# Encoder and decoder blocks in one kernel: conversions of the dilated stage in another order, cross attention without a row of token scales, its output in three split passes, squares taken earlier

## The reference, cut to what matters

```python
def first_block(x, mem, ...):                      # one layer
    q, k, v, u, y = split(rmsnorm(h, norm_mix_g) @ w_in)
    attn = dilated_mixture_attention(rope(q), rope(k), v)         # 8 heads of 64
    rec = bidirectional_rglru(conv(u), ...) * gelu(y)
    h = h + concat([attn, rec]) @ w_out
    h = h + memory_cross_attention(rmsnorm(h, norm_cross_g), rmsnorm(mem, norm_mem_g),
                                   w_cq, w_ck, w_cv, w_co)        # 4 heads of 128
    h = h + square(relu(rmsnorm(h, norm_mlp_g) @ w_mlp_in)) @ w_mlp_out
    return rmsnorm(h, norm_final_g)

def second_block(x, ...):                          # two layers
    o_mla, o_fnet, o_diff, o_hgrn = four mixers of rmsnorm(x, ln_mix) @ w_in
    x = x + (sum over n of sigmoid(gate_n) * (o_n @ w_branch[n])) @ w_out
    x = x + (silu(g) * u) @ w_down                 # g, u of rmsnorm(x, ln_ffn) @ w_gate_up
```

## Time and profile before

| | |
|---|---|
| median of three runs | 1317.44 us (1315.93 to 1322.8) |
| the profiled execution, its own time | 1320.47 us |
| its span in the profile | 1318.7 us |
| mean granted TensorE clock | 0.992 |
| TensorE busy | 1276.7 us, 97% of the span |
| VectorE busy | 863.5 us, 65% |
| ScalarE busy | 641.5 us, 49% |
| GpSimd busy | 116.6 us, 9% |
| DMA | 211.77 MB, mean 161 GB/s |

### The profile page before, as it was taken

How to read it: one execution, slowest core, us unless ns; L and a number is a source line. 1 busy time by engine, 2 the same in 40 slices (tenths; PEclk the granted TensorE clock), 3 DMA queues, 4 the chain that set the end, 5 groups by cost and what they waited for, 6 DMA issues and landing times.

```text
span 1318.7 us, 22038 instructions
## 1 busy us (share of the span) xinstructions
PE 1276.7 (97%) x9196; PEld 1179.6 (89%) x9196; DVE 863.5 (65%) x1206; ACT 641.5 (49%) x1027; POOL 116.6 (9%) x152
## 2 busy tenths in 40 slices
PE   8988989999999999999999999999999999999998
PEld 8986959998888889998999998898899988999986
DVE  6878547664466756799655554557576996655543
ACT  5865436553366655252364443548553433644432
POOL 2100100000000000481200000000002820000000
PEclk9998999999999999999999999999999999999999
DMA  9532515555543333342545555444334325455552
GB/s 374 212 105 97 192 36 208 202 181 187 184 170 144 140 117 131 130 157 79 209 160 183 179 185 189 166 154 150 106 130 155 133 96 185 143 186 190 192 192 96
DMA packets 30324, 211.77 MB, mean 161 GB/s; under 512 B 3344, under 2 KB 3728, under 8 KB 5264
## 3 DMA queue, kind: packets, MB, share of 16 engines
q1 hardware_dynamic: 29936, 210.22, 44.6%
...
q10 hardware_dynamic: 288, 0.14, 0.0%
...
## 4 chain that ended last, share of the span: by engine, by line
PE 70%; DVE 15%; ACT 8%; issue 6%; DMA 1%; DVEq 0%; ACTq 0%
PE bank L477 68%; DVE w_lo L1545 3%; ACT w_hi L1066 2%; DVE W L1519 2%; ACT W L1066 1%; DVE xs L2035 1%; PE bank L577 1%; ACT x_hi L1066 1%; DVE W L1505 1%; DMA ring<-weight_pieces 1%; DVE W L2015 1%; DVE junk L2033 1%; DVE W L1506 1%; PE bank L783 1%; DVE W L1537 0%
## 5 line engine op out<-in xcount | busy, mean ns | idle before, releaser
L1545 DVE TENSOR_TENSOR w_lo<-ring,w_hi 128x2048 fp32r<-128x2048 f32 (+1 forms) x181 | 418.1, 2310 | 294.8 <-ACT w_hi L1066 294.6
L1066 ACT ACTIVATE w_hi<-ring 128x1024 fp32r<-128x1024 f32 (+1 forms) x364 | 362.1, 1045 | 239.8 <-PE bank L477 224.0
L477 PE MATMUL bank<-x_hi,w_hi 128*128 128x256 f32 x1840 | 266.2, 283 | 2.7 <-ACT w_hi L1066 2.6
L477 PE MATMUL bank<-x_hi,w_lo 128*128 128x256 f32 x1840 | 261.1, 280 | 1.5 <-DVE w_lo L1545 0.9
L477 PE MATMUL bank<-x_lo,w_hi 128*128 128x256 f32 x1840 | 254.2, 280 | 0.0
L477 PEld LDWEIGHTS bank<-x_hi,w_hi 128*128 128x128 f32 x1840 | 236.2, 188 | 5.8 <-issue 2.9
L477 PEld LDWEIGHTS bank<-x_hi,w_lo 128*128 128x128 f32 x1840 | 235.9, 188 | 2.8 <-DVE w_lo L1545 1.7
L477 PEld LDWEIGHTS bank<-x_lo,w_hi 128*128 128x128 f32 x1840 | 233.1, 188 | 0.0
L477 PE MATMUL bank<-W 128*128 128x128 f32 (+4 forms) x716 | 113.4, 327 | 13.3 <-ACT W L1066 8.9
L477 PEld LDWEIGHTS bank<-W 128*128 128x128 f32 (+3 forms) x716 | 88.5, 187 | 28.2 <-issue 13.8
L477 PE MATMUL bank<-w_hi,hid_hi 128*128 128x512 f32 x304 | 78.5, 394 | 0.0
...
## 6 DMA issues: line engine op xcount, KB each, us to landing
...
```

Source lines behind the costliest of these rows:

```text
L477: return nc.tensor.matmul(out, lhsT, rhs, start=first, stop=last)
L1066: return nc.scalar.activation(out, in_, ACT.Copy, scale=scale)
L1545: v.tensor_tensor(w_lo[:, q % SPLITS, 0:n], raw(pp)[:, 0:n], w_hi[:, q % SPLITS, 0:n].bitcast(F32), ALU.subtract).then_inc(s_weight_low, 1)
```

## The change

1. Dilated stage. The low part of `v0`, and both parts of `mem_hi`, move ahead of `rgA 0`; the high part of `v1` stands behind `rgA 0`. `mem_lo` is made in two halves (`memlow`), one before the low part of `v1`, one before that of `ck0`. `memrs` moves behind head 0's mask and maximum. The conversions of `ck1`, `cv0`, `cv1` and `wout0` are each placed in the filler ahead of the projection in front of them, and `rgS`, `rgC 1` and `rgC 3` move to the end of their turn, behind these conversions. The multiplications of the probabilities move from VectorE to ScalarE (two copies with a scale).
2. Cross attention. No row of scales, no multiplication of `cq` by it: the scale of a token, with the constant, is the scale of the exponential and of the maximum. The two `cq` tiles are copied out of PSUM by ScalarE. The scores of heads 0 and 1 are made between the halves of `cq1`, and the four heads follow in an order written out by hand.
3. `co`. Both pieces are split like the others, the values are split into `x_hi` (ScalarE) and `x_lo` (VectorE), and each product is made in three passes of fp32r instead of one in float32: 48 multiplications of 128x512 for 16.
4. Squares. For the norms after `wout` and `co`, the squares of a column block of `h` are taken during the next projection; only the last block's stay behind the norm.
5. In the second block, the row of scales of `ln_ffn` is made behind `gu1` and not between its halves.

```diff
+                late = []
                 if filler and i >= first:
-                    steps.extend(filler.pop(0))
+                    now = filler.pop(0)
+                    if None in now:
+                        now, late = now[:now.index(None)], now[now.index(None) + 1:]
+                    steps.extend(now)
                 if not long:
                     steps.extend(turn)
                 if 3 <= i:
                     steps.append(("value", *heads[i - 3]))
+                steps.extend(late)
...
-        steps += [("low", k[1][-1]), ("rgI",), k[0], ("high", v[0][-1]), ("rgA", 0), k[1], ("high", v[1][-1]), ("rgA", 1), v[0], ("low", v[1][-1])]
         (ck0, ck1), (cv0, cv1) = proj("ck"), proj("cv")
-        steps += [("norm", "norm_mem_g"), ("high", ck0[-1]), ("low", ck0[-1]), v[1], ("memrs",)]
+        wouts = proj("wout", js=range(4))
+        steps += [("low", k[1][-1]), ("rgI",), k[0], ("high", v[0][-1]), ("low", v[0][-1]), ("norm", "norm_mem_g"), ("rgA", 0), k[1], ("memlow", 0)]
+        steps += [("high", v[1][-1]), ("low", v[1][-1]), v[0], ("high", ck0[-1]), ("memlow", 1), ("low", ck0[-1]), ("rgA", 1), v[1]]
         attend([("dil", n) for n in range(8)],
-               [[("rgB", 0), ck0], [("rgB", 1), ("rgS",)], [ck1], [("rgC", 0)], [("rgC", 1), cv0], [("rgC", 2)], [("rgC", 3), cv1], [("mix",)]], 1)
+               [[("memrs",)], [("high", ck1[-1]), ("rgB", 0), ("low", ck1[-1]), ck0], [("rgB", 1), None, ("rgS",)],
+                [("high", cv0[-1]), ("low", cv0[-1]), ck1], [("rgC", 0)], [("high", cv1[-1]), ("low", cv1[-1]), cv0, None, ("rgC", 1)],
+                [("rgC", 2)], [("high", wouts[0][-1]), ("low", wouts[0][-1]), cv1, None, ("rgC", 3)], [("mix",)]])
         mixes = (0, 1, "rec", 2, 3)
-        steps += proj("wout", js=range(4))
+        steps += wouts
         steps.append(("norm", "norm_cross_g"))
         steps += proj("cq")
-        attend([("cross", n) for n in range(4)])
-        steps += proj("co", n=0)
+        cross = lambda kind, n: (kind, "cross", n)
+        steps += [cross("score", 0), cross("score", 1), cross("prob", 0), ("cqcopy",), cross("turn", 0), cross("prob", 1), cross("score", 2),
+                  cross("turn", 1), cross("value", 0), cross("score", 3), cross("prob", 2), cross("value", 1), cross("turn", 2),
+                  cross("prob", 3), cross("value", 2), cross("turn", 3), cross("value", 3)]
+        steps += proj("co")
         steps.append(("norm", "norm_mlp_g"))
         ups = proj("up", js=range(16))
         steps += [*ups[:4], ("params",), *ups[4:]]
...
-                    middle = {"y0": "norm_mix_g", "cq1": "norm_cross_g", "gu1": f"ln_ffn_{l}"}.get(f"{name}{j}")
-                    if middle:
+                    if (name, j) == ("y", 0):
                         def between():
-                            rstd_row(middle)
+                            rstd_row("norm_mix_g")
+                    elif (name, j) == ("cq", 1):
+                        def between():
+                            for n in ("cq.0", "ck.0", "ck.1"):
+                                wait_drained(pe, n)
+                            scores([(ATT["cross", n][1], "cross", n, 0) for n in range(2)])
...
                     elif name == "co":
...
-                        plain(job, "g", at(A_CO, 4, S), loaded(p).rearrange("p (k c) -> p k c", k=4), range(4), 512, p)
+                        q = split_of[p]
+                        hi, lo = (w[:, q % SPLITS, :].rearrange("p (k c) -> p k c", k=4) for w in (w_hi, w_lo))
+                        pe.wait_ge(s_weight_high, 2 * (q + 1))
+                        for tt in range(TT):
+                            bank = fill(f"{job}.{tt}", "g")
+                            for i in range(2):
+                                for kk in range(4):
+                                    if j == tt == i == 0:
+                                        pe.wait_ge(s_co_high, kk + 1)
+                                    elif j == tt == 0:
+                                        wait_drained(pe, f"value.cross{kk}")
+                                    for w, x in ((hi, x_hi), (lo, x_hi)) if i == 0 else ((hi, x_lo),):
+                                        if w is lo and tt == kk == 0:
+                                            wait_low(pe, q)
+                                        ins = mm(bank[:, :], x[:, kk, tt * P:(tt + 1) * P], w[:, kk, :], i == kk == 0 and w is hi, i == 1 and kk == 3)
+                            full(ins, f"{job}.{tt}")
+                        last_job[p] = f"{job}.{TT - 1}"
...
+                    elif name == "gu" and j == 1:
+                        rstd_row(f"ln_ffn_{l}")
...
+                    if phase == "cross" and hd == 2:
+                        wait_drained(pe, "cq.1")
...
+                        if hd % 2 == 0:
+                            scores([(a0, phase, hd, 0), (a0 + 1, phase, hd + 1, 0)])
+                    elif phase != "cross" or hd >= 2:
+                        scores([(a0 + j, phase, hd, j) for j in range(count)])
...
                 elif p in split_of:
-                    split_ahead(p)
+                    split_ahead(p, step[1] not in ("ck", "cv"))
...
+                        squares(stat_name, {"norm_cross_g": (3,), "norm_mlp_g": (1,), "ln_ffn_0": (3,), "ln_ffn_1": (3,)}.get(stat_name, range(4)))
...
+                elif kind == "cqcopy":
+                    drains(copy(at(A_CQ, 4, S)[:, 2:4, :], bank2(wait_filled(act, "cq.1"))), "cq.1")
+                elif kind == "prob" and step[1] == "dil":
+                    a = ATT["dil", step[2]][1]
+                    p0, rs = at(A_SC1 + 512 * (a % 4), TT, S), col(f"rsum{a % 16}", TT)
+                    act.wait_ge(s_dil_recip, a + 1)
+                    copy(p0[:, 0, :], p0[:, 0, :], rs[:, 0:1])
+                    copy(p0[:, 1, :], p0[:, 1, :], rs[:, 1:2]).then_inc(s_prob, 1)
                 elif kind == "proj":
                     _, name, l, j, _ = step
                     job = job_of(name, l, j)
+                    if name == "wout" and j:
+                        squares("norm_cross_g" if l is None else f"ln_ffn_{l}", (j - 1,))
+                    elif name == "co" and j:
+                        squares("norm_mlp_g", (0,))
+                    elif name == "cq" and j == 0:
+                        drains(copy(at(A_CQ, 4, S)[:, 0:2, :], bank2(wait_filled(act, job))), job)
...
+                            token = col("rs.cross.scaled", TT)[:, qt:qt + 1] if phase == "cross" else scale
+                            ins = nc.scalar.activation(sc[:, qt, :], src[:, qt, :], ACT.Exp, bias=nm[:, qt:qt + 1], scale=token, accum_out=sm[:, qt:qt + 1])
...
-                        drains(copy(at(A_CO, 4, S)[:, hd, :], wait_filled(act, name)[:, 0:S]), name)
+                        copy(x_hi[:, hd, :], wait_filled(act, name)[:, 0:S]).then_inc(s_co_high, 1)
...
+                elif kind == "memlow":
+                    gain = vec[:, V_GAIN + GAINS.index("norm_mem_g") * KT:][:, 0:KT]
+                    for j in (2 * step[1], 2 * step[1] + 1):
+                        dve.wait_ge((s_norm_high, s_norm_high_dve)[j % 2], 2 + j // 2 + 1)
+                        for k in (2 * j, 2 * j + 1):
+                            ins = v.scalar_tensor_tensor(mem_lo[:, k, :], mem_t[:, k, :], gain[:, k:k + 1], mem_hi[:, k, :].bitcast(F32), ALU.mult, ALU.subtract)
+                        ins.then_inc(s_norm_low, 1)
...
+                        if name == "norm_cross_g":
+                            dve.wait_ge(s_rs, rs_of[name])
+                            link(v.tensor_scalar(col("rs.cross.scaled", TT), rs, 128.0 ** -0.5, None, ALU.mult))
...
+                    before = {"ck": "norm_mem_g", "f": f"ln_mix_{l}", "gu": f"ln_ffn_{l}"}.get(name)
+                    if before and j == (name == "gu"):
...
-                    elif name == "cq" and j == 1:
-                        for job in ("cq.0", "cq.1"):
-                            scale(at(A_CQ, 4, S)[:, 2 * int(job[-1]):2 * int(job[-1]) + 2, :])
...
+                elif kind == "value" and step[1] == "cross":
+                    hd = step[2]
+                    dve.wait_ge(s_co_high, hd + 1)
+                    bank = wait_filled(dve, f"value.cross{hd}")
+                    drains(v.tensor_tensor(x_lo[:, hd, :], bank[:, 0:S], x_hi[:, hd, :].bitcast(F32), ALU.subtract), f"value.cross{hd}")
...
+                            if phase == "cross":
+                                v.tensor_tensor(nm, mx, col("rs.cross.scaled", TT), ALU.mult).then_inc(s_max, 1)
...
+                    if phase == "dil":
+                        ins.then_inc(s_dil_recip, 1)
+                        continue
```

84 lines of the change are left out of this document (30 added, 54 removed).

## The result

The changed kernel takes 1327.15 us in the median of six runs (1325.71 to 1328.91), the kernel before 1317.28 beside it: ratio 1.0067, 95% interval 1.0046 to 1.0088, 9.9 us slower. Measured a second time, beside experiments and on another chip, it is 1.0056 (1.0034 to 1.0078), 7.4 us. The forecast was 1322.7 us, +5.3, with the range 1310 to 1329. The range holds and the sign is right. The size is too small, and the result lies beyond the half per cent, for which I had the chance 0.36 and not the largest one.

A forecast was written before the change was run, and what follows sets the result against it. TensorE, busy 97% of the span, bounds the kernel, with a ScalarE-VectorE ring pacing the dilated stage. Terms 9.9 - 5.2 - 3.0 + 3.6 = +5.3 us on the median 1317.4 gave 1322.7 us, range 1310 to 1329.

The forecast's parts named there:

- v1 and ck0: Start of the dilated stage: new wait of 0.9 us at v1, then ck0 without its 2.43 wait, ending 3.4 earlier.
- The gain is given back by 102: Dilated stage: TensorE, ahead by 3 us, waits for head 2's probabilities and starts head 1's values at 101.9 instead of 101.42.
- The ring: ScalarE and VectorE releasing each other in the dilated stage: head 6's mask 3.5 us late, last reciprocal 6.3, wout0 7.4.
- The sum of the stage: Whole dilated stage, late start of wout0 plus half clock: +9.9 us, between +7.4 and +11.5.
- Cross attention: Cross attention and co together: co starts 2.6 us earlier and itself takes 2.6 less, -5.2 us, between -7 and -3.5.
- one wait of 1.5 at head 2: Cross attention: the four heads run as before, with a single TensorE wait of 1.5 us, at head 2.
- Rows of `ln_ffn`: Row of scales in two layers: ready once made behind gu1, so the 1.5 us waits go, -3.0 us.
- Banks: Shifted bank rotation: new waits at the start of down (1.6 us) and each wd (1.0, twice), +3.6 us.
- Squares at nothing: Squares during wout and co: two more per projection on ScalarE cost nothing; without that cover about 1 us per block.
- break even: Rival: the dilated stage costs nothing because the ring has unseen slack; 1312.8 us, chance 0.20.
- nor gain: Rival: half-clock stretches and the wait at ck0 go from the dilated stage with nothing replacing them; 1308.9 us, chance 0.14.
- the clock case: Rival: dilated-stage waits leave TensorE at 1.2 GHz into wout0 and delay cv0; 1326.2 us, up to 1329, chance 0.20.

The follow-up runs named there:

- e5: Changed kernel with scans ahead of the conversions, probability scalings on VectorE and the old bank rotation, all put back: 1313.70 us, ratio 0.9952 to the kernel before.
- e7: e5 with the conversions of cv0, cv1 and wout0 one place further back: 1309.70 us, ratio 0.9917 to the kernel before.
- e1: Changed kernel with the dilated stage of the kernel before, the rest as changed: 1317.82 us, ratio 0.9986 to the kernel before.
- e2: Changed kernel with the third and last groups' scans ahead of the conversions of cv1 and wout0 again: 1320.88 us, ratio 1.0012 to the kernel before.
- e3: Changed kernel with the scalings of the dilated stage's probabilities on VectorE again: 1323.20 us, ratio 1.0026 to the kernel before.
- e8: Changed kernel with all squares behind their norms again: 1331.15 us, ratio 1.0090 to the kernel before.
- e4: Changed kernel with the rotation of the shared banks put back by one step ahead of up: 1322.64 us, ratio 1.0019 to the kernel before.

## Why the prediction was right, and where it was short

Times from the mark; first traces, where nothing else is said.

**v1 and ck0: right.** A new wait at `v1` of 0.68 us (0.9 forecast), first scores 1.1 us later (0.9), `ck0` without a wait. **The gain is given back by 102: right**, with the wait of 3.32 for about 3. I named the cause (`memrs` and the scalings) only in part: e5 shows that it is lost even with the scalings away, and e7 that it is kept once the conversions of `cv0`, `cv1` and `wout0` stand further back. At the low one of `cv0` VectorE stands for 8.17 us in the changed kernel (5.26 before).

**The ring: right.** Less the 1.8 of the start, head 6's mask is 3.9 us late (3.5 forecast), the last reciprocal 6.8 (6.3). `wout0` starts 8.7 late; the forecast is the ring's 7.4 and 1.9 for the last value products at half clock, 9.3. Those products cost 0.8 (2.65 us from start to start for 1.82), and the half clock in `wout0` 1.2 (0.6). So the ring was put too short and its clock too dear, by about half a us each, and the two cancel. The sum of the stage, forecast 9.9: 9.9 to `wout0`'s third pass (126.29 for 116.39), 9.5 by e1, and 8.7 in the second pair of traces (126.30 for 117.56). That one of them is 9.9 to the tenth is luck. e2 and e3 measure its two causes at 6.9 and 5.4 alone. They are not independent (12.3 in all), at least since each takes the half clock in `wout0`, 1.2, with it.

**Cross attention, forecast -5.2: -4.2.** `co` itself took 11.39 us (11.2). The step that was short is "one wait of 1.5 at head 2": there are five, 0.48, 0.54, 1.12, 0.75 and 0.75, so `co` starts 1.8 us earlier against `wout0`'s third pass and not 2.6 (47.43 us for 49.19, second traces; the first have 47.41 for 49.95, of which 0.8 is a slower `wout`, see the last section). That the scales come earlier and are needed is right: e8 takes it away and loses 3.0.

**Rows of `ln_ffn`, forecast -3.0: right**; the waits of 1.52 are gone in both layers. **Banks, forecast +3.6: +4.1** (1.81, 1.16, 1.16), and e4 shows the cause.

**Squares at nothing: right** for the projections; their worth lay in cross attention, where I had counted it.

**The sum.** With the stage of the first pair of traces the terms make 9.9 - 4.2 - 3.0 + 4.1 = 6.8, with that of the second 5.6, for a forecast of 5.3. The pairs themselves differ by 4.9 and 5.6 from the mark (some of it is how fast single projections ran), and by 6.7 and 5.7 in the times of the two executions. The medians gave 9.9 and 7.4. So the terms hold what the traces hold, and 2 to 3 us of the medians are in no trace: the profiled executions of the kernel before lay 3.2 and 2.5 us above its median. What its faster executions do otherwise was not traced, and executions of it spread from 1310.9 to 1325.5 us in one measurement.

One number on record points at the clock. Every execution lists its mean granted clock: 0.992 in the mean of 17 executions of the kernel before (0.990 to 0.996), 0.987 and 0.986 in the mean of the changed kernel's two times six (0.983 to 0.989). As an estimate, since a span at clock c has a share 2 x (1 - c) at half clock, that is 13 to 15 us more at half clock, at 0.5 each up to 6.5 to 7.5 us, where I had counted 2.5. The two profiled pairs differ by only 8 and 5 us of half clock. But what of it falls into waits costs nothing, so the clock is a candidate for the missing 2 to 3 us and not shown as their cause.

**The rivals.** The stage did not break even, nor gain. Of the clock case, one half came: after head 2's wait TensorE ran at half clock into `cv0` (granted clock 0.51 from 104 to 109 us, four products in 1.97 us). It did not reach head 6's mask, though, which was 0.4 us later than I had it and not 1.5, and at the end of the stage the half clock on the path cost 2.0 us for my 2.5. So in the traces that case is not what happened. The measured medians lie where it lay all the same, by 1.0 in cross attention, 0.5 in the banks, and the part that is in no trace. In so far it is luck that a case I had priced stands where the result is.

**Where it was short** is how the chances followed. The sum of +5.3 lay only 1.3 under the line at 6.6, with terms that may each be off by 1 us, and I gave 0.34 to two cases in which the stage breaks even or gains, though four exact orders stood against them. With less on these, "slower" would have had near half.
